# Interleaving the last two weight slabs of the token-major projections with the token tiles

## The chip, the cores and the metric

The kernel runs on one core of one Trainium2 chip. The metric is device time in microseconds (us), from the first to the last instruction of a launch with what lies around it. Engines are called PE (TensorE), DVE (VectorE), ACT (ScalarE), POOL (GpSimd) and SP (SyncE, which issues the weight DMAs).

## The reference

Sequence 512, width 1024, batch 1, all in float32. Two blocks run one after the other. The first has two layers, each of a mixer and a squared-ReLU MLP with a layer norm behind each:

```
for i in range(2):
    m = mixer_gdn(x) if i == 0 else mixer_gla(x)          # projections in, recurrence, projection out
    x = layernorm(ALPHA * x + m, ln1_g[i], ln1_b[i])
    h = relu(x @ mlp_w1[i])                               # 1024 -> 4096
    x = layernorm(ALPHA * x + (h * h) @ mlp_w2[i], ln2_g[i], ln2_b[i])
```

The second block is a gated mix of attention (with 256 context tokens) and multi-scale pooling, with its own projections in and out. What matters here are the four places where a projection back to width 1024 is added to x and normalised: behind the first mixer (a_out), the first MLP (down0), the second mixer (b_out) and the second MLP (down1). Behind the first three, the normalised x must be transposed and feeds the next projection (up0, b_qk, up1); behind down1 the second block starts.

## The kernel before, in words

**Arithmetic.** Every large product is made of three matmuls in a reduced float32 format, hi x hi, hi x lo and lo x hi (`mm3`, lines 261 to 265). A weight slab (128 partitions x 2048) is loaded by SP in two halves into `raw[0]` and `raw[1]`; ACT rounds each half into `whi[b]` (`split_hi`, line 248), then DVE subtracts to get `wlo[b]` (`split_lo`, line 254) and increments `w_ready`. There are two slab buffers, b = 0 and 1; ACT may fill one again when PE has used it (`slab_used`), and SP may fill a raw half again when DVE has read it.

**Two forms of product.** In the feature-major form (`pe_feature_slab`) the weights are stationary. In the token-major form (`pe_token_slab`) a tile of 128 tokens is stationary and the weights stream, 512 columns at a time; the 1024 output columns come in two halves. Each half has PSUM banks of its own, 0 to 3 for the first and 4 to 7 for the second, one bank per token tile (ST = 4). A slab holds 4 of the 128-row steps of the contraction, so one token tile on one slab is 4 x 3 = 12 matmuls of 512 columns. a_out and b_out have one pair of slabs for each half, down0 and down1 four (with the activations staged pair by pair by `act_stage` and `dve_stage`, line 454).

**The last pair.** The last pair of slabs of the second half is done by `pe_token_last` (line 320), token tile by token tile: slab 0 and then slab 1 for tile 0, the same for tile 1, and so on. When both slabs are through for a tile, PE increments `sum_ready` (for the last tile `slab_used`), and DVE adds the sum to X.

**The end of a layer on DVE and ACT.** `dve_token_layer` first adds the four tiles of the first half (`dve_add_half`, line 406) and takes their statistics (line 534); in a_out and b_out this stands behind the weight subtractions of the last pair, in down0 and down1 three pairs earlier. Then `dve_token_end` runs tile by tile: add (406), statistics (416, 418), the low part of the turned tile before (`dve_turned`, 398), and the two passes of the layer norm (427, 430), with the reciprocal deviation from ACT in between (436, 438). Before tile 3 it has the weight subtraction of the next layer's first slab:

```
            for st in range(1, ST):
                if st == 3:
                    split_lo(dve, nxt, 0)
                dve_norm_tile(dve, name, e, st, lambda: dve_turned(dve, e, st - 1))
```

ACT copies each turned tile from PSUM to `act_hi` (`act_turned`, line 390). After down1, there are no turns here; ACT makes the second block's own normalisation of each tile (lines 2242 to 2248), and PE turns that in `pe_c_turn` (line 2330).

**Turns.** PE transposes a normalised tile of X in eight 128 x 128 steps, two halves of four (`pe_turn_tile`, `pe_turn_half`, line 377), into the banks `TURN_BANK`. It waits for `x_ready` from DVE, and for tile 2, which goes to the banks of tile 1, also for DVE's low part of tile 1. Turns of tiles 0 to 2 stand in `turn_between`, behind the sums of tiles 1 to 3.

**The next layer's first slab.** `pe_feature_first` (line 1524) contracts the first slab of up0, b_qk or up1 as the tiles come: `part(j, kts, t0, t1)` is feature tile j, some of the 8 contraction steps, token tiles t0 to t1. First come all 8 steps on tokens of tiles 0 and 1 for j = 0 (in two halves, each waiting for its half of the weights), then j = 1 on tiles 0 to 2, with the two halves of the turn of tile 3 in between.

The order of each engine is the order in which its stream is written; only semaphores tie the engines together.

Of the kernel before, what the change touches and what calls it, by code (L numbers as in the profile page):

```python
# [26 lines left out]
ST = S // P  # L27
# [18 lines left out]
PH = {}  # L46
# [62 lines left out]
def build(nc, a, out):  # L109

    ctx = ExitStack()
    with ctx:
# [6 lines left out]
        whi = [sb(f"whi{i}", [P, SLAB], F32R) for i in range(2)]  # L119
        wlo = [sb(f"wlo{i}", [P, SLAB], F32R) for i in range(2)]  # L120
# [17 lines left out]
        bk = [ctx.enter_context(nc.psum_tensor(f"bk{i}", [P, 512], F32)) for i in range(8)]  # L138
# [4 lines left out]
        act_lo = sb("act_lo", [P, KT, S], F32R)  # L143
# [5 lines left out]
        act_hi = sb("act_hi", [P, KT, S], F32R)  # L149
# [26 lines left out]
        w_ready = sem("w_ready")  # L176
        hid_ready = sem("hid_ready")
        stage_hi_ready = sem("stage_hi_ready")
        stage_ready = sem("stage_ready")
        mix_hi_ready = sem("mix_hi_ready")  # L180
        mix_ready = sem("mix_ready")
        slab_used = sem("slab_used")
        acc_ready = sem("acc_ready")
        acc_free = sem("acc_free")
        sum_ready = sem("sum_ready")
# [44 lines left out]
        def slab_view(t, kts):  # L230
            return t[:, :].rearrange("p (k n) -> p k n", k=kts)
# [29 lines left out]
        def mm3(acc, lhs_hi, lhs_lo, rhs_hi, rhs_lo, first, last):  # L261

            nc.tensor.matmul(acc, lhs_hi, rhs_hi, start=first, stop=False, skip_group_check=True)  # L263
            nc.tensor.matmul(acc, lhs_hi, rhs_lo, start=False, stop=False, skip_group_check=True)  # L264
            return nc.tensor.matmul(acc, lhs_lo, rhs_hi, start=False, stop=last, skip_group_check=True)  # L265
# [51 lines left out]
        STAGED = {"down0": 0, "down1": 16}  # L317
        MIXED = {"a_out": 0, "b_out": 8, "c_out": 16}

        def pe_token_last(pe, name, pair0, first, between):  # L320

            for st in range(ST):
                tok = slice(st * P, st * P + P)
                for b in range(2):
                    if st == 0:
                        pe.wait_ge(w_ready, 2 * (PH[name][0] + 2 * pair0 + b + 1))
                        if PH[name][1] > 4:
                            pe.wait_ge(stage_ready, STAGED[name] + 2 * pair0 + b + 1)
                    hi, lo = slab_view(whi[b], 4), slab_view(wlo[b], 4)
                    for kt in range(4):  # L330
                        f = b * 4 + kt
                        mm = mm3(bk[4 + st][:, :], act_hi[:, f, tok], act_lo[:, f, tok], hi[:, kt, :], lo[:, kt, :],
                                 first and f == 0, f == 7)
                    if st == 3:
                        mm.then_inc(slab_used, 1)
                    elif b == 1:
                        mm.then_inc(sum_ready, 1)
                between(pe, st)

        def pe_token_layer(pe, name, between, middle=None, first=None, order=range(ST)):  # L340
            pairs = PH[name][1] // 4
# [21 lines left out]
        def pe_turn_tile(pe, e, name, st):  # L363

            if st == 0:
                pe.wait_ge(sum_added, 4 * (TH[name] + 1))
            for hf in range(2):
                pe_turn_half(pe, e, name, st, hf)

        def pe_turn_half(pe, e, name, st, hf):  # L370

            pe.wait_ge(x_ready, 8 * (e - 1) + 2 * st + (hf + 1 if st == 3 else 2))
            if st == 2:
                pe.wait_ge(act_ready, 8 * e + 2 + hf + 1)
            for k in range(4):
                kt = 4 * hf + k
                mm = nc.tensor.transpose(bk[TURN_BANK[st] + hf][:, k * P:k * P + P], X[:, st, kt * P:kt * P + P], eye[:, :])
            mm.then_inc(xt_ready, 1)

        def turn_between(name, e):  # L380
            def between(pe, st):
                if st >= 1:
                    pe_turn_tile(pe, e, name, st - 1)
            return between

        def act_turned(act, e, tiles=range(ST)):
# [791 lines left out]
        def pe_a_last(pe):  # L1178
            h = AH - 1
            pe_a_scan_new(pe, h, 0)  # L1180
            for cc in range(1, ST):
                pe_a_scan_state(pe, h, cc)
                pe_a_scan_new(pe, h, cc)
# [340 lines left out]
        def pe_feature_first(pe, name, before, e, middle=None):  # L1524

            hi, lo = slab_view(whi[0], KT), slab_view(wlo[0], KT)

            def part(j, kts, t0, t1):
                c, t = slice(j * P, j * P + P), slice(t0 * P, t1 * P)
                for kt in kts:  # L1530
                    mm = mm3(bk[j][:, t], hi[:, kt, c], lo[:, kt, c], act_hi[:, kt, t], act_lo[:, kt, t],
                             kt == 0 and t0 == 0, kt == KT - 1 and t1 == ST)
                return mm

            pe.wait_ge(acc_free, 2 * FS[name] - 2)
            pe.wait_ge(act_ready, 8 * e + 4)
            for hf in range(2):
                pe.wait_ge(w_ready, 2 * PH[name][0] + hf + 1)
                part(0, range(4 * hf, 4 * hf + 4), 0, 2)
            pe.wait_ge(act_ready, 8 * e + 6)  # L1540
            part(1, range(0, 6), 0, 3)
            pe_turn_half(pe, e, before, 3, 0)
            part(1, range(6, 8), 0, 3)
            pe_turn_half(pe, e, before, 3, 1)
            pe.wait_ge(act_ready, 8 * e + 7)
            part(0, range(0, 4), 2, 4)
            part(1, range(0, 4), 3, 4)
            pe.wait_ge(act_ready, 8 * e + 8)
            part(0, range(4, 8), 2, 4).then_inc(acc_ready, 1)
            if middle is not None:  # L1550
                middle(pe)
            part(1, range(4, 8), 3, 4).then_inc(slab_used, 1)
# [786 lines left out]
        def pe_c_turn(pe):  # L2339
            pe.wait_ge(K.sem, K.at("xn", 5))  # L2340
            for i in range(8, 16):
                pe_c_turn_one(pe, i)
# [627 lines left out]
        @block.tensor  # L2970
        def _(pe):
            pe_start(pe)
            pe_a_in(pe)
            for h in range(AH):
                pe_a_head(pe, h)
            pe_a_last(pe)
            pe_token_layer(pe, "a_out", turn_between("a_out", 1), None, pe_a_out_first)
            pe_up(pe, 0, "a_out", 1)
            pe_mod(pe, 0, "up0")
            pe_token_layer(pe, "down0", turn_between("down0", 2))  # L2980
            pe_b_in(pe)
            for h in range(BH):
                pe_b_head(pe, h)
            pe_token_layer(pe, "b_out", turn_between("b_out", 3), None, pe_b_out_first, (2, 3, 0, 1))
            pe_up(pe, 1, "b_out", 3)
            pe_mod(pe, 1, "up1")
            pe_token_layer(pe, "down1", lambda pe, st: None, pe_c_context_turn)
            pe_c_turn(pe)
            pe_c_in(pe)
            pe_c_attend(pe)  # L2990
            for half in range(2):
                for b in range(2):
                    pe_token_slab(pe, "c_out", half, 0, b, half, b == 0, b == 1)
# [24 lines left out]
```

## Time and profile before

| | |
|---|---|
| median of 3 runs | 1933.51 us (1931.22 to 1935.85) |
| the profiled execution, its own time | 1938.38 us |
| its span, first to last instruction | 1936.6 us |
| busy PE / DVE / ACT / POOL | 1850.2 / 984.4 / 731.5 / 238.8 us |
| mean granted clock of TensorE | 0.977 |
| instructions | 24200 |

The profile page gives busy times, the chain of waits that ended last, and groups of instructions; the trace behind it can be asked for the timeline of an engine in a window. Times in a timeline are us from the start of the span. A busy PE is not PE at its peak: matmuls are pipelined, so one that is listed with 0.39 us may be followed by the next after 0.23. The idle time in brackets is the time that the engine stood before the instruction, with the instruction that ended it.

### The profile page before, as it was taken

The page shows a single profiled execution, that of the slowest core. Times are in us where ns is not written, and L with a number is a line of the kernel's source. Part 1 is how long each engine was busy: PE and PEld are TensorE (multiplying, and loading weights), DVE is VectorE, ACT ScalarE, POOL GpSimd, SP SyncE. Part 2 cuts the span into 40 slices and gives each one's busy share as a digit, 9 for nine tenths or more (in the row PEclk, how much of TensorE's full clock was granted, in tenths as well). Part 3 has the DMA queues.
Part 4 walks back from the last instruction along what each step waited for, and adds up shares of the span by engine and source line. Part 5 has one row for each costly group of instructions (what it writes and reads, how often), then busy time and mean ns, then how long its engine had stood idle before and what let it go on. Part 6 is the DMA issues. An engine that isn't in the chain of part 4 may idle for free.

```text
span 1936.6 us, 24200 instructions
## 1 busy us (share of the span) xinstructions
PE 1850.2 (96%) x9152; PEld 1497.6 (77%) x9152; DVE 984.4 (51%) x1387; ACT 731.5 (38%) x1186; POOL 238.8 (12%) x225
## 2 busy tenths in 40 slices
PE   8999999999999999999998889999999997999989
PEld 7887788888788878887776777788878885775667
DVE  3775466666554443446321576654443566323653
ACT  3334555554232232332533344232323354344440
POOL 2001244442000000000000243000000000101500
PEclk8999999999999999999998999999999998999999
DMA  4233200000432233322222100442243231421001
GB/s 130 87 96 100 65 2 1 1 1 2 152 109 87 92 106 120 102 94 66 87 86 67 44 1 20 155 130 88 87 167 115 87 105 48 157 65 44 1 1 65
DMA packets 102034, 146.72 MB, mean 76 GB/s; under 512 B 4641, under 2 KB 70385, under 8 KB 101696
## 3 DMA queue, kind: packets, MB, share of 16 engines
q1 hardware_dynamic: 95472, 121.45, 19.8%
q0 software_dynamic: 6480, 24.13, 3.4%
q8 instruction: 57, 0.93, 0.2%
q14 instruction: 25, 0.20, 0.0%
HBM read 143.47 MB, written 2.10 MB: 75 GB/s over the span
## 4 chain that ended last, share of the span: by engine, by line
PE 88%; DVE 4%; ACT 3%; DMA 2%; issue 2%; POOL 1%; SPq 0%; ACTq 0%; DVEq 0%; POOLq 0%
PE bk L263 22%; PE bk L265 22%; PE bk L264 22%; PE bk L1049 2%; PE bk L1067 2%; PE bk L2688 1%; PE bk L2689 1%; PE bk L1058 1%; PE bk L1879 1%; PE bk L2708 1%; ACT whi L248 1%; PE bk L967 1%; PE bk L1038 1%; POOL work L1470 1%; POOL work L1851 1%
## 5 line engine op out<-in xcount | busy, mean ns | idle before, releaser
L254 DVE TENSOR_TENSOR wlo<-raw,whi 128x1024 fp32r<-128x1024 f32 x222 | 263.0, 1223 | 431.6 <-ACT whi L248 427.6
L263 PE MATMUL bk<-act_hi,whi 128*128 128x512 f32 (+3 forms) x1072 | 419.9, 392 | 1.6 <-DVE act_lo L2272 0.8
L264 PE MATMUL bk<-act_lo,whi 128*128 128x512 f32 (+3 forms) x1072 | 415.9, 388 | 0.0
L265 PE MATMUL bk<-act_hi,wlo 128*128 128x512 f32 (+3 forms) x1072 | 415.7, 388 | 0.0
L248 ACT ACTIVATE whi<-raw 128x1024 fp32r<-128x1024 f32 x222 | 224.6, 1053 | 319.4 <-PE bk L265 286.7
L263 PE MATMUL bk<-whi,act_hi 128*128 128x512 f32 x768 | 313.2, 408 | 23.9 <-DVE act_lo L454 12.0
L265 PE MATMUL bk<-whi,act_lo 128*128 128x512 f32 x768 | 310.4, 404 | 0.0
L264 PE MATMUL bk<-wlo,act_hi 128*128 128x512 f32 x768 | 308.8, 402 | 0.0
L263 PEld LDWEIGHTS bk<-act_hi,whi 128*128 128x128 f32 (+1 forms) x1072 | 202.2, 189 | 51.6 <-issue 5.1
L264 PEld LDWEIGHTS bk<-act_lo,whi 128*128 128x128 f32 (+1 forms) x1072 | 202.2, 189 | 45.3 <-issue 1.0
L265 PEld LDWEIGHTS bk<-act_hi,wlo 128*128 128x128 f32 (+1 forms) x1072 | 202.1, 189 | 45.4
L263 PEld LDWEIGHTS bk<-whi,act_hi 128*128 128x128 f32 x768 | 148.6, 194 | 62.1 <-issue 18.0
L264 PEld LDWEIGHTS bk<-wlo,act_hi 128*128 128x128 f32 x768 | 148.7, 194 | 37.0 <-issue 0.5
L265 PEld LDWEIGHTS bk<-whi,act_lo 128*128 128x128 f32 x768 | 148.2, 193 | 36.3
L1573 DVE TENSOR_TENSOR arena<-arena x64 | 44.3, 693 | 183.4 <-ACT arena L1560 183.2
L1560 ACT ACTIVATE arena<-bk 128x512 f32 x64 | 38.3, 598 | 246.4 <-PE bk L265 246.4
L1851 POOL TENSOR_TENSOR work<-work,arena 128x512 f32<-128x512 f32 x24 | 36.3, 1525 | 412.0 <-ACT work L1835 366.8
L454 DVE TENSOR_TENSOR act_lo<-arena,act_hi 128x2048 fp32r<-128x2048 f32 x32 | 73.2, 2292 | 13.9 <-ACT act_hi L448 13.9
L819 DVE SCALAR_TENSOR_TENSOR work<-work,convw 128x512 f32<-128x512 f32 x96 | 64.6, 746 | 0.0
L1049 PE MATMUL bk<-work 128*128 128x128 f32 x384 | 61.7, 283 | 1.4 <-DVE work L1386 1.2
L448 ACT ACTIVATE act_hi<-arena 128x2048 fp32r (+1 forms) x32 | 60.7, 1903 | 0.0
L1049 PEld LDWEIGHTS bk<-work 128*128 128x128 f32 x384 | 52.8, 192 | 9.6 <-issue 6.0
(384 smaller groups left out, 2336.5 us busy)
## 6 DMA issues: line engine op xcount, KB each, us to landing
raw<-in_mlp_w SPq DMA_DIRECT2D x128, 512.0 KB, 3.9
raw<-in_a_w_in SPq DMA_DIRECT2D x32, 512.0 KB, 4.2
work<-in_w_mod POOLq DMA_DIRECT2D x3, 4096.0 KB, 17.8
raw<-in_b_w_in SPq DMA_DIRECT2D x24, 512.0 KB, 4.5
raw<-in_w_in SPq DMA_DIRECT2D x14, 512.0 KB, 4.2
raw<-in_a_w_out SPq DMA_DIRECT2D x8, 512.0 KB, 4.6
raw<-in_b_w_out SPq DMA_DIRECT2D x8, 512.0 KB, 4.5
raw<-in_w_out SPq DMA_DIRECT2D x8, 512.0 KB, 4.1
```

Source lines behind the costliest of these rows:

```text
L248: nc.scalar.activation(whi[b][:, hs], raw[hf][:, :], ACT.Copy).then_inc(w_hi_ready, 1)
L254: nc.vector.tensor_tensor(wlo[b][:, hs], raw[hf][:, :], whi[b][:, hs], ALU.subtract).then_inc(w_ready, 1)
L263: nc.tensor.matmul(acc, lhs_hi, rhs_hi, start=first, stop=False, skip_group_check=True)
L264: nc.tensor.matmul(acc, lhs_hi, rhs_lo, start=False, stop=False, skip_group_check=True)
L265: return nc.tensor.matmul(acc, lhs_lo, rhs_hi, start=False, stop=last, skip_group_check=True)
L448: nc.scalar.activation(stage(act_hi, b), hid_group(pair, b), ACT.Copy).then_inc(stage_hi_ready, 1)
L454: nc.vector.tensor_tensor(stage(act_lo, b), hid_group(pair, b), stage(act_hi, b), ALU.subtract).then_inc(stage_ready, 1)
L819: nc.vector.scalar_tensor_tensor(out=acc, in0=src, scalar=wk, in1=acc, op0=ALU.mult, op1=ALU.add).then_inc(conv_step, 1)
L1049: mm = nc.tensor.matmul(bk[s][:, c % 2 * P:c % 2 * P + P], A["K"][:, c, :], z_right(l, c * P, P), start=True, stop=True, skip_group_check= ...
L1067: mm = nc.tensor.matmul(bk[s][:, (2 + c % 2) * P:(3 + c % 2) * P], A["X"][:, c, :], A["T"][:, c, :], start=True, stop=True, skip_group_che ...
L1573: nc.vector.tensor_tensor(tile, tile, tile, ALU.mult).then_inc(hid_ready, 1)
L1851: nc.gpsimd.tensor_tensor(halves(out, l), b_mix(b_slot(l), l, False), halves(b_kT[:, h, :], l), ALU.mult).then_inc(B["zk"], 1)
```

## The change

In the last pair the order of (slab, token tile) is written out as a table: slab 0 on tiles 0 and 1, slab 1 on tiles 0 and 1, and then slab 0 and slab 1 in turn on tile 2 and on tile 3. The callback `between` is called after each step and gets the slab as well; it turns tile 0 behind slab 0 on tile 2, and tile 1 behind slab 0 on tile 3. The turn of tile 2 moves into `pe_feature_first`, between its first two halves. In there, the first half of tile 3's turn comes after 4 contraction steps of feature tile 1 instead of 6, and the second half after 6 instead of 8. This holds at a_out, down0 and b_out; down1 has the new order without turns. The code of the other engines is the same.

```diff
@@ -317,25 +317,26 @@
         STAGED = {"down0": 0, "down1": 16}
         MIXED = {"a_out": 0, "b_out": 8, "c_out": 16}
 
+        LAST_ORDER = ((0, 0), (0, 1), (1, 0), (1, 1), (0, 2), (1, 2), (0, 3), (1, 3))
+
         def pe_token_last(pe, name, pair0, first, between):
 
-            for st in range(ST):
+            for b, st in LAST_ORDER:
                 tok = slice(st * P, st * P + P)
-                for b in range(2):
-                    if st == 0:
-                        pe.wait_ge(w_ready, 2 * (PH[name][0] + 2 * pair0 + b + 1))
-                        if PH[name][1] > 4:
-                            pe.wait_ge(stage_ready, STAGED[name] + 2 * pair0 + b + 1)
-                    hi, lo = slab_view(whi[b], 4), slab_view(wlo[b], 4)
-                    for kt in range(4):
-                        f = b * 4 + kt
-                        mm = mm3(bk[4 + st][:, :], act_hi[:, f, tok], act_lo[:, f, tok], hi[:, kt, :], lo[:, kt, :],
-                                 first and f == 0, f == 7)
-                    if st == 3:
-                        mm.then_inc(slab_used, 1)
-                    elif b == 1:
-                        mm.then_inc(sum_ready, 1)
-                between(pe, st)
+                if st == 0:
+                    pe.wait_ge(w_ready, 2 * (PH[name][0] + 2 * pair0 + b + 1))
+                    if PH[name][1] > 4:
+                        pe.wait_ge(stage_ready, STAGED[name] + 2 * pair0 + b + 1)
+                hi, lo = slab_view(whi[b], 4), slab_view(wlo[b], 4)
+                for kt in range(4):
+                    f = b * 4 + kt
+                    mm = mm3(bk[4 + st][:, :], act_hi[:, f, tok], act_lo[:, f, tok], hi[:, kt, :], lo[:, kt, :],
+                             first and f == 0, f == 7)
+                if st == 3:
+                    mm.then_inc(slab_used, 1)
+                elif b == 1:
+                    mm.then_inc(sum_ready, 1)
+                between(pe, b, st)
 
         def pe_token_layer(pe, name, between, middle=None, first=None, order=range(ST)):
             pairs = PH[name][1] // 4
@@ -378,9 +379,9 @@
             mm.then_inc(xt_ready, 1)
 
         def turn_between(name, e):
-            def between(pe, st):
-                if st >= 1:
-                    pe_turn_tile(pe, e, name, st - 1)
+            def between(pe, b, st):
+                if b == 0 and st >= 2:
+                    pe_turn_tile(pe, e, name, st - 2)
             return between
 
         def act_turned(act, e, tiles=range(ST)):
@@ -1537,11 +1538,14 @@
             for hf in range(2):
                 pe.wait_ge(w_ready, 2 * PH[name][0] + hf + 1)
                 part(0, range(4 * hf, 4 * hf + 4), 0, 2)
+                if hf == 0:
+                    pe_turn_tile(pe, e, before, 2)
             pe.wait_ge(act_ready, 8 * e + 6)
-            part(1, range(0, 6), 0, 3)
+            part(1, range(0, 4), 0, 3)
             pe_turn_half(pe, e, before, 3, 0)
+            part(1, range(4, 6), 0, 3)
+            pe_turn_half(pe, e, before, 3, 1)
             part(1, range(6, 8), 0, 3)
-            pe_turn_half(pe, e, before, 3, 1)
             pe.wait_ge(act_ready, 8 * e + 7)
             part(0, range(0, 4), 2, 4)
             part(1, range(0, 4), 3, 4)
@@ -2984,7 +2988,7 @@
             pe_token_layer(pe, "b_out", turn_between("b_out", 3), None, pe_b_out_first, (2, 3, 0, 1))
             pe_up(pe, 1, "b_out", 3)
             pe_mod(pe, 1, "up1")
-            pe_token_layer(pe, "down1", lambda pe, st: None, pe_c_context_turn)
+            pe_token_layer(pe, "down1", lambda pe, b, st: None, pe_c_context_turn)
             pe_c_turn(pe)
             pe_c_in(pe)
             pe_c_attend(pe)
```

PE at a_out, where slab 1 comes in (bk4 to bk7 are the banks of token tiles 0 to 3, whi0 and wlo0 slab 0, whi1 and wlo1 slab 1). Before:

```order
L264 MATMUL bk4<-wlo0,act_hi 128x512
L265 MATMUL bk4<-whi0,act_lo 128x512
L263 MATMUL bk4<-whi1,act_hi 128x512 [waits w_ready]
L264 MATMUL bk4<-wlo1,act_hi 128x512
L265 MATMUL bk4<-whi1,act_lo 128x512
```

and now:

```order
L264 MATMUL bk5<-wlo0,act_hi 128x512
L265 MATMUL bk5<-whi0,act_lo 128x512
L263 MATMUL bk4<-whi1,act_hi 128x512 [waits w_ready]
L264 MATMUL bk4<-wlo1,act_hi 128x512
L265 MATMUL bk4<-whi1,act_lo 128x512
```

The wait for slab 1 stood behind the first 12 matmuls; now it stands behind 24, of which the last 12 go to bk5, tile 1.

PE at a_out, the turn of tile 0 (into bk0 and bk1). Before:

```order
L265 MATMUL bk5<-whi1,act_lo 128x512
L377 MATMUL bk0<-eye,X 128x128 [waits x_ready,sum_added]
L377 MATMUL bk0<-eye,X 128x128 x3
L377 MATMUL bk1<-eye,X 128x128 [waits x_ready]
L377 MATMUL bk1<-eye,X 128x128 x3
L263 MATMUL bk6<-whi0,act_hi 128x512
L264 MATMUL bk6<-wlo0,act_hi 128x512
```

and now:

```order
L265 MATMUL bk6<-whi0,act_lo 128x512
L378 MATMUL bk0<-eye,X 128x128 [waits x_ready,sum_added]
L378 MATMUL bk0<-eye,X 128x128 x3
L378 MATMUL bk1<-eye,X 128x128 [waits x_ready]
L378 MATMUL bk1<-eye,X 128x128 x3
L263 MATMUL bk6<-whi1,act_hi 128x512
L264 MATMUL bk6<-wlo1,act_hi 128x512
```

The turn stood ahead of slab 0 on tile 2 (bk6); it now stands behind it and ahead of slab 1.

PE at the passage from a_out to up0 (bk0 with 256 columns is feature tile 0 on token tiles 0 and 1). Before:

```order
L265 MATMUL bk7<-whi1,act_lo 128x512
L377 MATMUL bk2<-eye,X 128x128 [waits act_ready,x_ready]
L377 MATMUL bk2<-eye,X 128x128 x3
L377 MATMUL bk3<-eye,X 128x128 [waits act_ready,x_ready]
L377 MATMUL bk3<-eye,X 128x128 x3
L263 MATMUL bk0<-act_hi,whi0 128x256 [waits w_ready,act_ready,acc_free]
L264 MATMUL bk0<-act_lo,whi0 128x256
```

and now:

```order
L264 MATMUL bk0<-act_lo,whi0 128x256
L265 MATMUL bk0<-act_hi,wlo0 128x256
L378 MATMUL bk2<-eye,X 128x128 [waits act_ready,x_ready]
L378 MATMUL bk2<-eye,X 128x128 x3
L378 MATMUL bk3<-eye,X 128x128 [waits act_ready,x_ready]
L378 MATMUL bk3<-eye,X 128x128 x3
L263 MATMUL bk0<-act_hi,whi0 128x256 [waits w_ready]
L264 MATMUL bk0<-act_lo,whi0 128x256
```

The turn of tile 2 (bk2 and bk3) stood ahead of the first matmul of up0, which waits for the new weights; it now stands 12 matmuls behind that wait.

## Rows read from the trace of the kernel before

**Rows 1.** The page: busy time of the engines, and the chain that ended last.

```profile
PE 1850.2 (96%) x9152; PEld 1497.6 (77%) x9152; DVE 984.4 (51%) x1387; ACT 731.5 (38%) x1186; POOL 238.8 (12%) x225
...
PE 88%; DVE 4%; ACT 3%; DMA 2%; issue 2%; POOL 1%; SPq 0%; ACTq 0%; DVEq 0%; POOLq 0%
```

**Rows 2.** The list of waits of PE: who for whom, us in total, times, longest.

```profile
PE bk L263 <- DVE act_lo L454: 12.0, 4, 3.7
...
PE bk L263 <- DVE wlo L254: 6.1, 2, 3.8
```

**Rows 3.** Timeline of PE, a_out's end: start, us, engine, line, operation, idle before.

```profile
505.80 0.39 PE L263 MATMUL bk<-whi,act_hi 128*128 128x512 f32 x1
...
511.05 0.79 PE L263 MATMUL bk<-whi,act_hi 128*128 128x512 f32 x1 [2.28 <-DVE wlo L254]
...
521.08 1.03 PE L377 MATMUL bk<-eye,X 128*128 128x128 f32 x8
...
534.04 1.04 PE L377 MATMUL bk<-eye,X 128*128 128x128 f32 x8
534.83 0.37 PE L263 MATMUL bk<-act_hi,whi 128*128 128x256 f32 x1
...
540.86 0.60 PE L377 MATMUL bk<-eye,X 128*128 128x128 f32 x4
...
542.87 0.39 PE L263 MATMUL bk<-act_hi,whi 128*128 128x256 f32 x1
```

**Rows 4.** Stretches: us, busy PE, PEld, DVE, ACT, POOL; granted clock, DMA share, GB/s.

```profile
505.80:508.60 2.80, 2.80 (x13) 2.06 (x11) 1.23 (x1) 1.06 (x1) 0.00 (x0) 1.00 0.66 250
...
511.00:514.50 3.50, 3.45 (x8) 2.78 (x9) 3.47 (x6) 0.00 (x0) 0.00 (x0) 0.51 0.67 204
...
1153.60:1158.00 4.40, 4.31 (x28) 4.18 (x28) 3.86 (x8) 1.81 (x3) 3.02 (x3) 1.00 0.00 0
```

**Rows 5.** Timeline of PE at the same place of down0 and b_out.

```profile
890.17 0.77 PE L263 MATMUL bk<-whi,act_hi 128*128 128x512 f32 x1 [3.70 <-DVE act_lo L454]
...
1227.99 0.80 PE L263 MATMUL bk<-whi,act_hi 128*128 128x512 f32 x1 [3.79 <-DVE wlo L254]
```

**Rows 6.** Timeline of DVE, a_out's end.

```profile
509.76 1.23 DVE L254 TENSOR_TENSOR wlo<-raw,whi 128x1024 fp32r<-128x1024 f32 x1 [1.39 <-ACT whi L248]
...
515.80 0.67 DVE L406 SCALAR_TENSOR_TENSOR X<-X,bk 128x512 f32<-128x512 f32 x1
...
519.41 1.28 DVE L430 SCALAR_TENSOR_TENSOR X<-X,rstd,work 128x1024 f32<-128x1024 f32 x1
521.28 0.69 DVE L406 SCALAR_TENSOR_TENSOR X<-X,bk 128x512 f32<-128x512 f32 x1 [0.59 <-PE bk L265]
...
525.39 1.29 DVE L430 SCALAR_TENSOR_TENSOR X<-X,rstd,work 128x1024 f32<-128x1024 f32 x1
...
533.07 2.35 DVE L254 TENSOR_TENSOR wlo<-raw,whi 128x1024 fp32r<-128x1024 f32 x2
...
535.94 1.28 DVE L398 TENSOR_TENSOR act_lo<-bk,act_hi 128x512 fp32r<-128x512 f32 x2
...
539.35 0.75 DVE L430 SCALAR_TENSOR_TENSOR X<-X,rstd,work 128x512 f32<-128x512 f32 x1
```

**Rows 7.** Timeline of ACT, a_out's end.

```profile
521.72 1.08 ACT L390 ACTIVATE act_hi<-bk 128x512 fp32r<-128x512 f32 x2 [3.81 <-PE bk L377]
```

**Rows 8.** Timeline of DVE, the first add of down0 and of b_out.

```profile
894.68 0.69 DVE L406 SCALAR_TENSOR_TENSOR X<-X,bk 128x512 f32<-128x512 f32 x1 [4.66 <-PE bk L265]
...
1232.75 0.67 DVE L406 SCALAR_TENSOR_TENSOR X<-X,bk 128x512 f32<-128x512 f32 x1
```

**Rows 9.** Timelines of DVE and PE, down1's end.

```profile
1613.93 0.68 DVE L406 SCALAR_TENSOR_TENSOR X<-X,bk 128x512 f32<-128x512 f32 x1
...
1640.66 5.58 PE L2330 MATMUL bk<-eye,arena 128*128 128x128 f32 x28 [10.51 <-ACT arena L2248]
```

**Rows 10.** Timeline of PE, a short wait in the second mixer.

```profile
1153.69 1.13 PE L1879 MATMUL bk<-work 128*128 128x128 f32 x8 [1.05 <-POOL work L1851]
```

## The prediction, made before the change was run

> **What bounds the kernel now.** I read the chain of waits on the page first: 88% of the span on TensorE (PE), 4% on VectorE (DVE), 3% on ScalarE (ACT) [rows 1]. So only stretches where PE stands still, or runs slowly, are to be had. The list of waits then gives two large ones on the three matmuls of line 263: for the low part of an activation and of a weight slab, both from DVE [rows 2]. In the timeline of PE I looked up where they lie. One kind opens each of the four contractions that the change touches: the last pair of a_out, down0, b_out and down1, at the step from slab 0 to slab 1.
>
> At a_out the pair starts at 505.80; its first 12 matmuls (one token tile on one slab, a "unit" below) take 2.80 us [rows 4]; then PE stands until 511.05, and the note says DVE, the weight subtraction [rows 3]. That is 511.05 - 508.60 = 2.45 us lost. PE then runs at a granted clock of 0.51, that is 1.2 instead of 2.4 GHz, for some 3.5 us [rows 4]. From 511.05 to 521.08 there are three units, 8.4 us of work in 10.0: 1.6 us lost to the clock. Down0 and b_out show waits of 3.70 and 3.79 us at the same place (in down0, as in down1, for the staged activations of slab 1, which DVE makes behind its weights) [rows 5], so with the clock these three ends lose 4.1, 5.3 and 5.4 us on PE, and down1 about as much.
>
> But what follows is not PE's alone. The normalisation of each token tile runs on DVE, and its rows show how little room there is: tile 1 begins at 521.28 and its last step, of 1.29 us, at 525.39, so 5.3 us in all before DVE is free again (its instructions overlap by some 0.1); behind tile 2 stands the weight subtraction for the next layer's first slab at 533.07, two halves in 2.35 us, so 1.2 for the first [rows 6]. PE takes that half up at 534.83, right behind the turn of tile 2 (0.79 us) [rows 3]. It was ready at 534.3: **0.5 us of slack**. So DVE is a second path beside PE through this whole stage, and nearly as long.
>
> **The change, part by part, at a_out.** No instruction is added or removed, on any engine; PE's order alone changes.
>
> *Second slab one unit later.* PE reaches slab 1 at 505.80 + 2 x 2.80 = 511.40 instead of 508.60. It may start at 511.05, so wait and slow clock go, and the units end 514.20, 517.00, 519.80 (tiles 0, 1 and slab 0 of tile 2).
>
> *What DVE makes of it.* Its add of tile 0 stays at 515.80 [rows 6], because the four adds and four statistics of the first half are queued ahead on DVE. Tile 0 is normalised at 519.41 + 1.28 = 520.69. The turn of tile 0, which before came at 521.08, is now asked for at 519.80: **a new wait of 1.0 us** to 520.8. Then come the turn (0.79) and two units to 527.2, the turn of tile 1 to 528.0, and the last unit to 530.8. DVE gains the 0.67 us that it waited for tile 1: its add goes to 520.6, and tile 2 starts at 525.9. But PE turns tile 1 only at 527.2, one unit behind the sum of tile 2; ACT starts its copy 0.64 us behind a turn (521.08 to 521.72) and needs 0.6 for the first half [rows 3, 7], so DVE waits about 1.0 for the low part of tile 1. The weight subtraction starts at 525.9 + 5.3 + 1.0 = 532.2 instead of 533.07.
>
> *First slab of the next layer.* PE is there at 530.8, the first half of the weights at 533.5. **A new wait of 2.7 us.** What the early second slab gave is paid back here.
>
> *Turn of tile 2 moved behind the first half.* After 533.5 come 12 matmuls of 256 columns (1.4 us) and then the turn, at 534.9; before it stood at 534.04 [rows 3]. DVE's low part of tile 2, before at 535.94 [rows 6], waits for turn, 0.64 and 0.6: 536.2, so 0.3 later, and all of tile 3 with it. Its first half is ready at 539.35 + 0.75 + 0.3 = 540.4. PE, with only 12 matmuls of 384 columns (2.1 us) put ahead of that turn, waits from 539.5 to 540.5, and behind it still has 12 such matmuls where 6 were left before: 1.04 us more. Before, 2.01 us lay between this turn and the next part (540.86 to 542.87) [rows 3]; now 540.5 + 2.01 + 1.04 = 543.5 less some 0.1 of overlap: 543.4. **A_out ends 0.5 later**, although 4.1 us of standstill at its head are gone.
>
> *b_out* has the same queue on DVE: the add of tile 0 at 1232.75 is held by the first half's adds there too [rows 8]. The wait at slab 1 shrinks to 3.79 - 2.80 = 1.0 to 1.2 us. Result as a_out: 0.5 later.
>
> *down0* has no such queue: DVE's add of tile 0 (894.68) [rows 8] waited for PE, whose unit ran at 1.2 GHz. The wait for slab 1 shrinks from 3.70 to 0.9 to 1.1, and slab 1 still cannot begin before 890.17 [rows 5]. If the clock stays up, the sum of tile 0 comes 1.5 us earlier, and everything behind with it: -1.5, and less of DVE's other slack, since the reordering costs the same 0.5 as above: about -0.8.
>
> *down1* has no turns. DVE's add of tile 0 is held at 1613.93 by DVE's own work, and PE waits 10.5 us for ACT before 1640.66 [rows 9]: PE ends its units earlier and waits longer. Zero.
>
> *The clock.* A wait of about 1 us is seen at 1153.69, with a granted clock of 1.00 behind it [rows 4, 10]: the shortened waits at slab 1 cost no clock. The new wait of 2.7 us is nearest to the 2.28 of a_out, behind which the clock fell [rows 3, 4]. Lower end nothing (as behind 1.05 us), upper end 1.6 us an end, as priced above. Part of the slow stretch will fall where PE waits for DVE anyway, so I take 1.0 an end: +3.0. The Trainium skill (page "TensorE: Matmul & The Clock Gate", section "Why this matters for your kernels") warns only of idle gaps longer than either of these; by it the new wait would cost no clock, and the sum would be +0.2. This trace speaks against that, by the 0.51 behind a wait of 2.28 us.
>
> **Sum:** 0.5 + 0.5 - 0.8 + 0 + 3.0 = +3.2 us. Against the profiled execution (1938.38 us, 4.9 above the median) that is 1941.6; the sum is a difference, so on the median of 1933.51 it is **1936.7 us**. About 0.2%, or 3.9 us, is what a measurement of this kernel can tell from no change: its three runs lie 4.6 us apart.
>
> **Rivals.**
> *PE's path decides after all (faster).* If DVE has more slack than I find, PE keeps what it saves at the slabs: 4.1 at a_out, 5.3 - 1.0 at down0, 5.4 - 1.1 at b_out, in all -12.7: 1920.8. For it: 88% of the chain on PE. Against: 0.5 us of slack at 533.07. The same comes from a rule in the Trainium skill (page "Perfetto Trace Analysis", section "Identifying the Most-Contended Engine"), to work on the busiest engine first; occupancy says PE here, the rows at this place say DVE. Chance 0.12, with the half-way cases.
>
> *The new wait keeps the clock down for longer (slower).* Within 7 us, between 530.8 and 540.5, PE would wait 2.7, 0.3 and 1.0 us. If that holds 1.2 GHz over two stretches like the one of [rows 4], the matmuls behind the wait delay the turn of tile 2, and with it DVE: 2 x 1.6 at three ends and 0.2 is +9.8: 1943.3. It decides if the waits of 0.3 and 1.0 us, harmless alone, act together with the one of 2.7. For it: they stand close together. Against: behind the wait of 2.28 us the clock was back at full after 3.5 us [rows 4]. Chance 0.13.
>
> *The change does not do what it says.* PE would find slab 1 late again. The order of PE's instructions shows that the wait for it now stands behind two units, so I give this nothing of its own.
>
> **How the numbers follow.** My forecast has 0.75. Its bounds are the clock's (nothing to 4.8) and about 1.5 us for the hand-made schedule, so 1932.2 to 1940.0; about two thirds of it lies within 0.2% (up to 1937.4), a third above. With the rivals: faster 0.12, same 0.51, slower 0.37. The range goes a little beyond the forecast's own, to hold eight in ten: 1929 to 1941.
>
> **What the changed profile would show.** Right: no wait at slab 1 in a_out, about 1 us in the other three, no slow clock behind it; PE waiting some 1 us for the turn of tile 0 in a_out and b_out; a wait of 2.5 to 2.9 us on DVE's weight subtraction at the first matmul of up0, b_qk and up1, with a slow stretch at most of these; the wait before down1's turned tiles grown from 10.5 to 14 or more. Wrong: if DVE's weight subtraction starts less than 1.5 us behind the end of the pair, the chain on DVE was misread; if no slow clock follows the new wait, 3.0 of the sum is gone.

## The result

| | before | changed |
|---|---|---|
| median | 1933.51 us | 1939.39 us |
| lowest to highest | 1931.22 to 1935.85 | 1937.49 to 1941.46 |
| profiled execution: span | 1936.6 us | 1936.5 us |
| mean granted clock | 0.977 | 0.981 |

Seven runs of each; the ratio is 1.003, with a 95% interval of 1.0019 to 1.0042. The change costs 5.9 us, some 3.7 to 8.1. The two profiled executions are of the same length, but the one of before (1938.38 us) was 4.9 us above its kernel's median and the changed one (1938.29) 1.1 us below its own. So the whole span tells nothing here; the stages do, and they are compared one by one below. Four executions of the experiments, of 2309 to 7681 us, stand far off all others, and the ratios leave them out.

The page of the changed kernel, the lines that answer to [rows 1]:

```profile
PE 1847.4 (95%) x9152; PEld 1497.1 (77%) x9152; DVE 984.6 (51%) x1387; ACT 730.4 (38%) x1186; POOL 237.8 (12%) x225
...
PE 85%; DVE 6%; ACT 3%; issue 2%; DMA 2%; POOL 1%; SPq 0%; ACTq 0%; DVEq 0%; POOLq 0%
```

TensorE's share of the chain went from 88% to 85%, VectorE's from 4% to 6%. The waits of PE, the ones that changed (who for whom: us in total, times, longest):

```profile
PE bk L2334 <- ACT arena L2252: 14.9, 1, 14.9
PE bk L263 <- DVE wlo L254: 8.8, 4, 2.6
...
PE bk L263 <- DVE act_lo L455: 5.4, 4, 2.3
...
PE bk L378 <- DVE X L431: 3.6, 5, 1.1
```

Against [rows 2], the wait for activations (now line 455) has fallen from 12.0 to 5.4 us and its longest from 3.7 to 2.3. The wait for weights has risen from 6.1 in two to 8.8 in four. A wait for the normalised X is new (3.6 us), and the one ahead of the turned tiles behind down1 has grown from 10.5 to 14.9. What went at the last pair stands again elsewhere. Timeline of PE at the end of a_out (start, us, engine, line, operation, idle before), to be held against [rows 3]:

```profile
521.45 1.06 PE L378 MATMUL bk<-eye,X 128*128 128x128 f32 x8 [1.04 <-DVE X L431]
...
527.95 1.04 PE L378 MATMUL bk<-eye,X 128*128 128x128 f32 x8
...
534.36 0.51 PE L263 MATMUL bk<-act_hi,whi 128*128 128x256 f32 x1 [2.56 <-DVE wlo L254]
...
537.02 1.43 PE L378 MATMUL bk<-eye,X 128*128 128x128 f32 x8
...
542.92 0.66 PE L378 MATMUL bk<-eye,X 128*128 128x128 f32 x4 [0.51 <-DVE X L431]
...
545.96 0.28 PE L263 MATMUL bk<-act_hi,whi 128*128 128x256 f32 x1
```

There is no wait at slab 1 any more. There is one of 1.04 us ahead of the turn of tile 0, and one of 2.56 us ahead of the first matmul of up0, for the weight subtraction. The waits at slab 1 and at the next layer's first weights, in down0 and then in b_out:

```profile
893.10 0.47 PE L263 MATMUL bk<-whi,act_hi 128*128 128x512 f32 x1 [0.90 <-DVE act_lo L455]
...
914.47 0.36 PE L263 MATMUL bk<-act_hi,whi 128*128 128x256 f32 x1 [2.59 <-DVE wlo L254]
...
1230.84 0.50 PE L263 MATMUL bk<-whi,act_hi 128*128 128x512 f32 x1 [1.07 <-DVE wlo L254]
...
1253.57 0.36 PE L263 MATMUL bk<-act_hi,whi 128*128 128x256 f32 x1 [2.57 <-DVE wlo L254]
```

DVE at a_out's end, against [rows 6]:

```profile
516.40 0.67 DVE L407 SCALAR_TENSOR_TENSOR X<-X,bk 128x512 f32<-128x512 f32 x1
...
521.22 0.68 DVE L407 SCALAR_TENSOR_TENSOR X<-X,bk 128x512 f32<-128x512 f32 x1
...
533.00 2.35 DVE L254 TENSOR_TENSOR wlo<-raw,whi 128x1024 fp32r<-128x1024 f32 x2
...
538.68 1.29 DVE L399 TENSOR_TENSOR act_lo<-bk,act_hi 128x512 fp32r<-128x512 f32 x2 [2.73 <-ACT act_hi L391]
```

The subtraction starts at 533.00. DVE then waits 2.73 us for ACT's copy of tile 2, whose turn PE could only make at 537.02. In stretches of 3.5 us behind the new wait at the three ends (the one in b_out begins 1.0 us behind the end of the wait; us, busy engines, then granted clock, DMA share, GB/s):

```profile
534.30:537.80 3.50, 3.44 (x16) 3.47 (x17) 1.65 (x2) 0.00 (x0) 0.00 (x0) 0.52 0.59 174
914.40:917.90 3.50, 3.43 (x29) 3.46 (x30) 2.30 (x4) 1.08 (x2) 0.00 (x0) 1.00 0.59 169
1254.60:1258.10 3.50, 3.50 (x19) 3.50 (x18) 1.35 (x3) 1.19 (x2) 0.00 (x0) 0.51 0.85 260
```

The clock was down at a_out and b_out (0.52, 0.51), not at down0 (1.00).

**Stage by stage.** This table goes from the first matmul of the last pair to the first matmul of the next layer's second slab (before, at a_out: 505.80 to 548.44; in down0 the small gate product of the next layer is inside it, up to the product that follows it). "slow" marks a stage in which the clock fell to about half behind a wait.

| kernel | a_out | down0 | b_out |
|---|---|---|---|
| before | 42.64 slow | 49.55 slow | 44.08 slow |
| changed | 45.19 slow | 49.21 | 46.17 slow |
| changed, second profile (e0) | 44.76 slow | 50.34 slow | 44.98 |
| e1 turn 2 back | 41.59 | 47.41 | 43.27 |
| e2 old order, turn 2 moved | 44.14 slow | 52.27 slow | 45.75 slow |
| e3 wait filled | 43.53 | 49.13 | 44.33 |
| e4 down1 only | 42.51 slow | 49.51 slow | 44.16 slow |
| e5 short subtraction | 43.68 slow | 48.36 | 44.31 |
| e6 turn 1 earlier | 40.74 | 46.18 | 41.94 |
| e7 early adds | 39.43 | 46.17 | 40.68 |
| e8 early adds alone | 41.47 | 49.72 slow | 44.15 slow |
| e9 early adds alone, again | 41.42 | 49.64 slow | 44.23 slow |
| e10 as e7, again | 39.46 | 46.11 | 40.77 |

Down1 gives nothing: from DVE's add of tile 0 (1613.93 [rows 9], now 1617.88) to the turned tiles (1640.66, now 1644.63) it is 26.7 us in both. The three ends of the changed kernel sum to 4.3 us more than before in one profile and 3.8 in the other.

Stretches that no version edits move as much from one profile to the next. The last pair of a_out begins between 505.80 and 510.01 us. In the two profiles of the changed kernel, 288.4 and 284.9 us lie between down0's end and b_out's last pair, and 666.3 and 671.6 us between b_out's end and the end of the span.

### The profile page after: what moved, and what is told of

It reads as the page before. It is cut to its first block, busy times and chain, and to the rows that moved or that the text cites. A ratio compares the mean times of both kernels' runs of the same rounds, so it can differ in the third digit from the quotient of the medians.

```text
span 1936.5 us, 24200 instructions
## 1 busy us (share of the span) xinstructions
PE 1847.4 (95%) x9152; PEld 1497.1 (77%) x9152; DVE 984.6 (51%) x1387; ACT 730.4 (38%) x1186; POOL 237.8 (12%) x225
## 4 chain that ended last, share of the span: by engine, by line
PE 85%; DVE 6%; ACT 3%; issue 2%; DMA 2%; POOL 1%; SPq 0%; ACTq 0%; DVEq 0%; POOLq 0%
PE bk L263 21%; PE bk L265 21%; PE bk L264 21%; PE bk L1050 2%; PE bk L1068 2%; PE bk L1059 1%; PE bk L2692 1%; PE bk L2693 1%; PE bk L1883 1%; PE bk L2712 1%; ACT whi L248 1%; DVE wlo L254 1%; DVE X L428 1%; DVE X L431 1%; PE bk L968 1%
```

## The experiments

Theory: at these ends the normalisation on DVE is a second path, as long as PE's; what PE saves at slab 1 comes back as a wait for the next layer's first weights, behind which the clock can fall, and the moved turn of tile 2 makes DVE's path longer. Each kernel was timed in five rounds against before.

**e0: the change again.**

> The change as it is, so that the edits below have it on the same chip. Theory (the chain on DVE sets the end of each layer; what PE saves at slab 1 comes back as a wait for the next layer's first weights, behind which the clock may fall): 5.9 us above before, as first measured, 3 to 8. Rival 1 (most of the 5.9 was chance in the clock): within 2 us of before.

Median 1937.85 against 1933.36; ratio 1.0011 (0.9997 to 1.0026). By the medians that is 4.5 us, by the ratio 2.1, and its interval reaches from no change to 5.0: of the same sign as at first, but smaller, and alone it would not show a loss. Both intervals hold 3.7 to 5.0 us. The three ends of its trace are longer by 3.8.

**e1: new order, the turn of tile 2 back.**

```diff
                 if b == 0 and st >= 2:
                     pe_turn_tile(pe, e, name, st - 2)
+                if b == 1 and st == 3:
+                    pe_turn_tile(pe, e, name, 2)
...
                 part(0, range(4 * hf, 4 * hf + 4), 0, 2)
-                if hf == 0:
-                    pe_turn_tile(pe, e, before, 2)
             pe.wait_ge(act_ready, 8 * e + 6)
-            part(1, range(0, 4), 0, 3)
+            part(1, range(0, 6), 0, 3)
             pe_turn_half(pe, e, before, 3, 0)
-            part(1, range(4, 6), 0, 3)
-            pe_turn_half(pe, e, before, 3, 1)
             part(1, range(6, 8), 0, 3)
+            pe_turn_half(pe, e, before, 3, 1)
```

> The new order of slabs and tiles, but the turn of tile 2 at the end of the pair and the first slab of the next layer exactly as before. Theory: the wait of 2.6 us for the weights breaks into 1.6 us for tile 2, its turn (0.8) and 0.3 us, so DVE gets tile 2's copy about 2.8 us earlier than in the change (where the clock fell) and no longer waits for it. PE then reaches the turn of tile 3 some 1.0 us earlier than in the kernel before at a_out and b_out, 2.5 at down0: 4.5 us faster than before, 10 faster than the change. Rival 1 (the interleaving of slabs is what costs, by its new waits, wherever the turn stands): 4 to 6 us slower than before, like the change. Rival 2 (PE's path decides): 12 us faster than before.

Median 1929.25, ratio 0.9975 (0.9963 to 0.9987): 4 to 5 us faster than before, 9 than the change. PE at a_out's end in e1:

```profile
531.30 1.04 PE L378 MATMUL bk<-eye,X 128*128 128x128 f32 x8
...
536.50 1.09 PE L378 MATMUL bk<-eye,X 128*128 128x128 f32 x8 [1.34 <-DVE X L433]
537.72 0.36 PE L263 MATMUL bk<-act_hi,whi 128*128 128x256 f32 x1
...
543.80 0.60 PE L378 MATMUL bk<-eye,X 128*128 128x128 f32 x4
```

PE waits 1.34 us for tile 2, turns it, and starts on up0 at 537.72. That is 1.22 us behind the start of the turn, where 0.79 was enough in before [rows 3], so some 0.4 us of waiting for the weights is left. The turn costs nothing there, because PE had to wait for these weights in any case. The clock fell at none of the three ends. Both rivals fall: the interleaving by itself gains, but 4, not 12.

**e2: the other half of the change alone.** The order of slabs and tiles of before, with `pe_feature_first` as in the change.

```diff
-        LAST_ORDER = ((0, 0), (0, 1), (1, 0), (1, 1), (0, 2), (1, 2), (0, 3), (1, 3))
+        LAST_ORDER = ((0, 0), (1, 0), (0, 1), (1, 1), (0, 2), (1, 2), (0, 3), (1, 3))
...
-                if b == 0 and st >= 2:
-                    pe_turn_tile(pe, e, name, st - 2)
+                if b == 1 and 1 <= st <= 2:
+                    pe_turn_tile(pe, e, name, st - 1)
```

> The other half of the change alone: the old order of slabs and tiles, with the turn of tile 2 behind the first half of the next layer's first tile and the halves of tile 3's turn after 4 and 6 steps. Theory: the turn of tile 2 is 1.8 us later than before, DVE's low part of it 1.1 us later, with it tile 3; and 1.04 us of matmuls stand behind the turn of tile 3 that stood ahead of it. 1.4 us at each of three ends: 4.3 us slower than before, with waits of PE of at most 1 us and no slow clock there. Rival 1 (the interleaving costs, the moved turn does not): within 1 us of before.

Median 1941.52, ratio 1.0033 (1.0021 to 1.0046): 8 us slower by the medians, 6.4 by the ratio; 4.3 was expected. The three ends of its trace sum to 5.9 more. A_out and b_out show it without another cause, 1.5 and 1.7 us longer (1.4 expected); down0 is 2.7 longer, with twice the slow stretch: behind the wait of 3.70 us at slab 1 the granted clock stayed at half for some 6.8 us. Behind the new, short waits there was no slow clock, as expected. PE at a_out's end:

```profile
536.17 0.35 PE L263 MATMUL bk<-act_hi,whi 128*128 128x256 f32 x1 [0.23 <-DVE wlo L254]
...
537.68 1.04 PE L378 MATMUL bk<-eye,X 128*128 128x128 f32 x8
...
543.18 0.66 PE L378 MATMUL bk<-eye,X 128*128 128x128 f32 x4 [0.54 <-DVE X L431]
```

The weights come almost in time (0.23), the turn of tile 2 stands 1.5 behind, and tile 3 is waited for.

**e3: the new wait filled with work.**

```diff
             pe.wait_ge(act_ready, 8 * e + 4)
+            for i in range(10):
+                nc.tensor.matmul(bk[0][:, :], act_hi[:, 0, 0:P], act_hi[:, 0, :], start=True, stop=True, skip_group_check=True)
             for hf in range(2):
```

> The change with ten more matmuls of 512 columns (2.33 us) ahead of the first half of the new weights, into a bank that is overwritten behind them, at the three ends where the new wait of 2.6 us stands: they fill the wait and do not lengthen it. Theory: the clock stays at 2.4 GHz behind it, DVE gets the turned tile 2 up to 1.6 us earlier: 2 to 4 us faster than the change, that is 2 to 4 us above before. Rival 3 (the clock has no part in it): the same as the change, 5.9 us above before.

Median 1933.66, ratio 0.9999 (0.9986 to 1.0012): as before, and faster than the change, by 2 us if the ratio of e0 is taken, 4 by its median, 6 by the first ratio. That is so although PE does 30 matmuls more. PE at a_out's end, and the clock behind the filler at the three ends:

```profile
533.60 2.47 PE L1539 MATMUL bk<-act_hi 128*128 128x512 f32 x10
536.25 0.38 PE L263 MATMUL bk<-act_hi,whi 128*128 128x256 f32 x1 [0.18 <-DVE wlo L254]
```

```profile
536.20:539.70 3.50, 3.45 (x29) 3.45 (x30) 2.40 (x4) 1.09 (x2) 0.00 (x0) 1.00 0.60 171
913.90:917.40 3.50, 3.44 (x29) 3.45 (x30) 2.40 (x4) 1.09 (x2) 0.00 (x0) 1.00 0.60 171
1248.00:1251.50 3.50, 3.42 (x29) 3.43 (x30) 2.39 (x5) 1.09 (x2) 0.00 (x0) 1.00 0.56 163
```

Of the 2.6 us only 0.18 is left, and the clock is at 1.00 everywhere. The three ends sum to 3.1 to 3.6 us less than in the change's two profiles. Some 0.6 of this is of another kind: in b_out PE waited 0.43 us at slab 1 here, where it waited 1.02 and 1.07 in the change. The rest stands where the clock fell in the change, so the clock is a real part of the change's loss.

**e4: the new order at down1 alone.**

```diff
-            for b, st in LAST_ORDER:
+            for b, st in (LAST_ORDER if name == "down1" else PLAIN_ORDER):
```

The turns and `pe_feature_first` are those of before; `PLAIN_ORDER` is the order of before.

> The new order at down1 alone; a_out, down0, b_out and the first slabs of the next layers as before. Theory (DVE's and ACT's chain sets the end of down1): the wait at slab 1 falls from 3.7 to 0.9 us and the wait ahead of the turned tiles grows from 10.5 to about 14.9 us; the time is that of before, within 1.5 us. Rival 2 (PE's path decides): 4 us faster.

Median 1934.22, ratio 1.0003 (0.9993 to 1.0013): no difference. The PE row that shows why, to be held against the 10.51 of [rows 9]:

```profile
1638.41 3.89 PE L2332 MATMUL bk<-eye,arena 128*128 128x128 f32 x17 [14.85 <-ACT arena L2250]
```

**e5: a shorter subtraction.** On the change, DVE subtracts only 256 of 1024 columns in each half of the first slab of up0, b_qk and up1; the other low parts stay as an earlier slab left them.

```diff
-                nc.vector.tensor_tensor(wlo[b][:, hs], raw[hf][:, :], whi[b][:, hs], ALU.subtract).then_inc(w_ready, 1)
+                nc.vector.tensor_tensor(wlo[b][:, hs], raw[hf][:, 0:256], whi[b][:, hs], ALU.subtract).then_inc(w_ready, 1)
```

(with `hs` cut to 256 columns, and used at that one place)

> The change, with the weight subtraction that the new wait is for (first slab of up0, b_qk and up1) cut to the first 256 of 1024 columns of each half; the other low parts of these three slabs are left as an earlier slab's. Theory: it sets the start of the next layer, so the first half is there 0.9 us earlier and the new wait is 1.7 instead of 2.6 us; turn of tile 2 and all behind it move up by 0.9 at each of three ends, and the clock falls there less often: 3 to 5 us faster than the change, 0 to 3 above before. Rival (ACT's rounding or the DMA of these weights sets it): the new wait stays at 2.6 and the time that of the change.

Median 1934.69, ratio 1.0003 (0.9990 to 1.0016): 2 us (by the ratio of e0) to 5 (by the first ratio) faster than the change; 3 to 5 was expected. The wait is 1.78 us now, 0.8 less, as forecast (0.9):

```profile
534.86 0.36 PE L269 MATMUL bk<-act_hi,whi 128*128 128x256 f32 x1 [1.78 <-DVE wlo L260]
```

So DVE's subtraction sets it, not ACT's rounding or the DMA. Its wait of 1.78 was still followed by the slow clock at a_out, and not at the other two ends (1.78 and 1.76).

**e6: as e1, the turn of tile 1 earlier.**

```diff
+                    if (b, st, kt) == (0, 3, 1):
+                        between(pe, b, st)
...
-                between(pe, b, st)
+                if (b, st) != (0, 3):
+                    between(pe, b, st)
```

> As e1_turn2_back, and the turn of tile 1 in the middle of slab 0 on tile 3 instead of behind it, 1.4 us earlier. Theory (DVE's chain is the bound, and it waits 1.0 us for tile 1's copy): that wait goes, tile 2 is normalised 1.0 us earlier, and PE's wait for it falls from 1.35 to some 0.4 us, at each of three ends: 3 us faster than e1, 7.5 below before. Rival 2 (after e1 PE's path decides): the same as e1, 4.5 below before.

Median 1927.91, ratio 0.9967 (0.9952 to 0.9982): 5.4 to 6.4 us below before, 7.5 expected; the three ends of its trace sum to 7.4 less, 3.4 less than e1's. At a_out PE turns tile 2 at 532.34, with no idle time listed, where e1 had 1.34:

```profile
532.34 1.09 PE L381 MATMUL bk<-eye,X 128*128 128x128 f32 x8
```

**e7: as e6, the first half's adds early.**

```diff
-                for b in range(2):
-                    split_lo(dve, next_pair(name, 0), b)
-            for st in range(ST):
-                dve_add_half(dve, name, 0, st)
-            dve.wait_ge(sum_added, 4 * TH[name] + 4)
-            for st in range(ST):
-                nc.vector.bn_stats(stats[:, st, 0, :], X[:, st, 0:512]).then_inc(st_stats, 1)
+                split_lo(dve, next_pair(name, 0), 0)
+                for st in range(ST):
+                    dve_add_half(dve, name, 0, st)
+                    dve.wait_ge(sum_added, 4 * TH[name] + st + 1)
+                    nc.vector.bn_stats(stats[:, st, 0, :], X[:, st, 0:512]).then_inc(st_stats, 1)
+                split_lo(dve, next_pair(name, 0), 1)
```

(down0 and down1 keep the old lines)

> As e6_turn1_earlier, and on DVE the adds and statistics of the first half (5 us) stand ahead of the weight subtraction of the last slab in a_out and b_out, where DVE is idle, instead of behind it. Theory: DVE's add of tile 0 no longer waits for them and comes 1.4 (a_out) and 1.7 us (b_out) earlier, PE's wait of 0.9 to 1.1 us for the turn of tile 0 goes, and of the rest 0.5 us is met by PE: 2 to 3 us faster than e6, 10 below before. Rival: the weight subtraction is pushed back by the adds, PE waits longer at slab 1, and e7 is not faster than e6.

Median 1922.72, ratio 0.9942 (0.9925 to 0.9958): 11 us faster than before, and 5 faster than e6, where 2 to 3 was expected. The three ends of its trace sum to 10.0 less than before and 2.6 less than e6's; where the other 2 us came from is open. DVE and PE at a_out's end in e7:

```profile
506.18 0.69 DVE L412 SCALAR_TENSOR_TENSOR X<-X,bk 128x512 f32<-128x512 f32 x1 [1.38 <-PE bk L265]
...
507.51 1.21 DVE L254 TENSOR_TENSOR wlo<-raw,whi 128x1024 fp32r<-128x1024 f32 x1
509.95 1.23 DVE L254 TENSOR_TENSOR wlo<-raw,whi 128x1024 fp32r<-128x1024 f32 x1 [1.24 <-ACT whi L248]
514.58 0.69 DVE L412 SCALAR_TENSOR_TENSOR X<-X,bk 128x512 f32<-128x512 f32 x1 [3.40 <-PE bk L265]
...
530.33 1.22 DVE L254 TENSOR_TENSOR wlo<-raw,whi 128x1024 fp32r<-128x1024 f32 x1
```

```profile
519.97 1.03 PE L381 MATMUL bk<-eye,X 128*128 128x128 f32 x8
...
525.17 1.09 PE L381 MATMUL bk<-eye,X 128*128 128x128 f32 x8
...
530.47 0.77 PE L381 MATMUL bk<-eye,X 128*128 128x128 f32 x5
```

The adds fill idle time of DVE. The pair begins at 505.98 here, so the first half of slab 1's subtraction (507.51) comes under 0.2 us later than in before and the second (509.95) at the same time. Tile 0's add waits for PE at 514.58, not PE for DVE, and none of the three turns has idle time listed ahead of it. DVE's weight subtraction still sets the start of up0: it begins at 530.33, its first half takes 1.22, and PE's first matmul of up0 stands at 531.70, which is 1.23 behind the start of the turn where 0.79 was enough in before.

**e8 and e9: these early adds alone, on the kernel before** (the diff of e7; everything on PE as before). The first:

> The kernel before with the early adds of e7 alone: old order of slabs, old turns, old first slab. Theory (PE and DVE take turns as the bound): with the old order the sum of tile 0 comes only 0.1 to 0.3 us before DVE is free for it, so an earlier free DVE has nothing to add; PE has no wait for DVE between slab 1 and the turn of tile 3. Within 1 us of before. Rival (the early adds are worth their 3 us by themselves, whatever the order): 2 to 4 us faster than before.

Median 1937.34 against 1933.30, ratio 1.0014 (1.0001 to 1.0028): a miss by its time, 3 to 4 us slower where nothing was expected. But at the three ends its trace has no stage that is more than 0.2 longer. It is 4 us behind the trace of before already at the end of the first 50 us, ahead of anything that was edited, and the traces of e1 and e10, whose kernels are faster, are as late there. The profiled execution was also the slowest of its twelve (1941.72). So it was run again:

> e8_early_adds_alone once more, since its time (0.14% above before, interval from 0.01%) and its trace (no stage longer than before) do not agree. Theory: the excess was chance, this time within 2 us of before. Rival: it is real, 3 to 5 us above before again, and there must be a cost outside the stages looked at.

Median 1936.00 against 1933.48, ratio 1.0010 (1.0000 to 1.0020): 2.5 us slower by the medians and 1.9 by the ratio, between the theory's 2 us and the rival's 3. The ends of its trace sum to 1.0 less than before, all of it at a_out, where this time the clock did not fall behind the wait at slab 1:

```profile
511.37 0.49 PE L263 MATMUL bk<-whi,act_hi 128*128 128x512 f32 x1 [2.60 <-DVE wlo L254]
...
519.87 0.38 PE L377 MATMUL bk<-eye,X 128*128 128x128 f32 x2
```

From 511.37 to 519.87 there are the same three units that took 10.0 us in before. What is clear: by themselves the adds are not worth what they bring on top of e6 (2.6 us by the traces, 5 by the times). Both e8 and e9 came out slower than before, with intervals that begin at no change or just above it; whether the adds cost 2 to 3 us in the mean, and where, is open.

**e10: e7 again.**

> e7_early_half0_adds once more, on the same chip as e9: 10 us below before by the theory, 8 to 12.

Median 1923.62 against 1933.48, ratio 0.9947 (0.9934 to 0.9960): 10 us. This version beats both kernels.

## Why the prediction was right, and where it was off

The time lay in the range, 1936.7 forecast and 1939.39 measured, and the likeliest case was the right one: +3.2 forecast, +5.9 at first and +4.5 in e0.

*DVE as a second path.* Right. The instants at a_out, with 0.44 taken off the trace's so that both pairs begin at 505.80:

| | forecast | measured |
|---|---|---|
| DVE adds tile 0 | 515.8 | 515.96 |
| turn of tile 0 | 520.8, wait 1.0 | 521.01, wait 1.04 |
| turn of tile 1 | 527.2 | 527.51 |
| DVE's weight subtraction for up0 | 532.2 | 532.56 |
| first matmul of up0 | 533.5, wait 2.7 | 533.92, wait 2.56 |
| turn of tile 2 | 534.9 | 536.58 |
| DVE's low part of tile 2 | 536.2 | 538.24 |
| first half of the turn of tile 3 | 540.5 | 542.48 |
| next part (tiles 2 and 3) | 543.4 | 545.52 |

Up to the first matmul of up0 the forecast is 0.2 to 0.4 early; behind it stands the slow clock, which the forecast had as a term of its own. E5 shows by shortening it that the subtraction sets that instant.

*The terms without the clock* were too small: +0.5, +0.5 and -0.8 were forecast, in sum +0.2. Where the clock did not fall, the ends measured +0.9 (a_out, e3), +0.9 (b_out, e0) and -0.3 (down0), in sum +1.5. The step that failed is the claim that PE would start the turn of tile 3 some 0.4 us earlier than before (540.5 against 540.86): it came at the same distance from the start of the pair as before, 35.0 us at a_out in e3 (35.1 before) and 36.5 at b_out in e0 (36.5 before). What stands behind that turn was forecast rightly: 0.93 us longer than before in e3, where 1.04 less 0.1 was expected. The 0.3 us that the forecast of that turn was early are a sum of small pieces. At a_out 0.16 were there already at DVE's add of tile 0, behind a subtraction whose slab had come that much later than in before (ACT waited 1.71 us for its DMA, 1.55 in before); 0.1 lay between the turns of tiles 0 and 1 (6.50 us against 6.4); the rest is under 0.1 at each hand-over.

*The clock.* Forecast 1.0 at each end, 3.0 in all. Measured from ends with and without a fall: 1.7 and 1.2 at a_out (45.19 and 44.76 against 43.53), 1.1 at down0 (50.34 against 49.21), 1.2 at b_out (46.17 against 44.98), at four ends of six in the two profiles: 2.6 us a run. E3 agrees with it: without any fall its ends sum to 3.1 to 3.6 us less than the change's, some 0.6 of which is the shorter wait at b_out's slab 1. The two parts together, 1.5 and 2.6, make 4.1 us, which is what the ends show (4.3 and 3.8); the 5.9 of the first measurement is more, and its interval begins at 3.7. The rule of the Trainium skill (page "TensorE: Matmul & The Clock Gate", section "Why this matters for your kernels"), by which only longer gaps do harm, would have left +0.2; the falls behind 2.56 us and less speak against it.

*down0* -0.8 forecast, -0.3 measured; *down1* zero, and zero (e4). *The sign of a misread chain* (DVE's weight subtraction less than 1.5 us behind the end of the pair) tells nothing: the forecast's own schedule has 1.4 (530.8 to 532.2), and 1.4 was measured. *The moved turn of tile 2*: the prediction put the blame on both halves of the change together; e1 and e2 part them. Interleaving gains 4 us, the moved turns lose 6 or more.

*The rivals.* PE's path did not decide: e1 keeps 4 of the 12.7 us. The longer slow stretch (+9.8) did not come in the change. One of that length is seen in e2 (down0, 6.8 us), but behind the old wait of 3.70 us, not behind a row of short ones.

## What to carry to other kernels

When a wait on the busiest engine is removed, lay out beside it the chain of the engine that it will meet next, instant by instant, and count the slack at each hand-over: here it was 0.5 us, so of the 12.7 us that PE seemed to have at hand the new order alone kept 4, and with the moved turns it came to a loss. Work that can only be late on the second chain (the turn of a tile that another engine needs) belongs ahead of a wait that comes anyway, not behind it. Then the second chain itself is worth shortening: moving one turn on PE, and adds on DVE into its idle time, brought 6 us more. The adds alone, in the old order, brought nothing.

## What was not expected of the hardware

How often the clock falls behind a wait of PE grows with the wait, over these traces. Behind the waits of 3.69 to 3.91 us at slab 1 (before, e2, e4, e8, e9) the slow clock came in 14 of 14 places. Behind waits of 2.3 to 2.7 us, with dense matmuls ahead of them, it came in 7 of 11 (as at 511.05 in before, behind 2.28) and not in the other 4 (as at 511.37 in e9, behind 2.60). Behind 1.8 us (e5) it came in 1 of 3, and behind 0.9 to 1.35 us at these ends never. It need not fall at once: in b_out of the changed kernel the granted clock was still 1.00 in the first 0.9 us behind the wait. A fall behind the new wait cost 1.1 to 1.7 us. So the same kernel's stage differs by over 1 us from run to run, and the stretches between the stages, where nothing was edited, by up to 5; single profiles cannot be compared by their span.
